# One ring of cells, held six tiles for U and seven for V instead of five and eight

## What is computed

```python
x = x + concat(RMSNorm(stick_breaking), RMSNorm(short_conv)) @ w_out
q1, q2 = split((RMSNorm(x) @ w_q) per head)            # 8 heads
s1, s2 = q1 @ sub_keys[0].T, q2 @ sub_keys[1].T        # 128 scores each
v1, i1 = top_k(s1, 16); v2, i2 = top_k(s2, 16)
top_s, pos = top_k(v1[:, None] + v2[None, :], 16)      # of 256 sums
idx = (i1 * 128 + i2)[pos]; gate = softmax(top_s)
act = gelu(sum_d expert_u[idx] * h)                    # one dot a pick
out = sum over picks of gate * act * expert_v[idx]
```

## Time and profile before

| what | us |
|---|---|
| median of the three runs | 2880.5 |
| the profiled execution, its own time | 2880.65 |
| its span (first to last instruction) | 2878.9 |
| POOL idle ahead of its DMAs, until a dot | 1372.7 |
| POOL idle ahead of its DMAs, until a mixed pair | 239.6 |
| PE, DVE, ACT, POOL busy | 2228.8, 1984.7, 1094.8, 1091.0 |

### The profile page before, as it was taken

How to read it: one execution, slowest core, us unless ns; L and a number is a source line. 1 busy time by engine, 2 the same in 40 slices (tenths; PEclk the granted TensorE clock), 3 DMA queues, 4 the chain that set the end, 5 groups by cost and what they waited for, 6 DMA issues and landing times. The chain is left out here.

```text
span 2878.9 us, 29484 instructions
## 1 busy us (share of the span) xinstructions
PE 2228.8 (77%) x9210; PEld 1015.9 (35%) x9210; DVE 1984.7 (69%) x4782; ACT 1094.8 (38%) x3164; POOL 1091.0 (38%) x1037
## 2 busy tenths in 40 slices
PE   9788989878987887778886888777898655555555
PEld 6535625433542343333442244333354111111111
DVE  3757766787666667787767666888676666666654
ACT  2323423562333336562333334666243332222232
POOL 0232423343333334443443333555333433333332
PEclk9999999889998998889998899999999787777786
DMA  9899999999999999999999999999999999999998
GB/s 389 331 418 404 402 420 418 417 412 410 394 421 421 419 419 399 421 421 419 409 422 421 420 411 418 404 414 418 418 412 421 417 422 421 420 420 417 419 416 353
DMA packets 178861, 1183.86 MB, mean 411 GB/s; under 512 B 19856, under 2 KB 21520, under 8 KB 47632
## 3 DMA queue, kind: packets, MB, share of 16 engines
q0 software_dynamic: 147456, 1073.81, 90.3%
q1 hardware_dynamic: 31248, 108.17, 9.5%
HBM read 1177.70 MB, written 4.19 MB: 411 GB/s over the span
## 5 line engine op out<-in xcount | busy, mean ns | idle before, releaser
L1470 DVE CUSTOM_DVE_ANT_0 ring<-ring,h2r 128x1024 f32<-128x1024 f32 x1024 | 1248.5, 1223 | 775.5 <-DMA ring<-table_uv,idx_t 768.3
L641 POOL DMA_INDIRECT ring<-table_uv,idx_t x1024 | 1089.1, 1064 | 1768.1 <-DVE dots L1470 1372.7
L909 PE MATMUL acc<-ring,wmask 128*64 128x512 f32 x4096 | 1202.2, 716 | 582.3 <-ACT wmask L1067 581.9
L909 PEld LDWEIGHTS acc<-ring,wmask 128*64 128x64 f32 x4096 | 283.2, 153 | 1293.3 <-ACT wmask L1067 856.5
L1062 ACT ACTIVATE dots<-dots 128x2 f32<-128x2 f32 x512 | 104.0, 203 | 1518.7 <-DVE dots L1470 1515.7
L1067 ACT ACTIVATE wmask<-gmask,dots 128x64 f32<-128x64 f32 x1024 | 300.4, 340 | 48.6 <-ACT dots L1062 1.5
L1055 ACT ACTIVATE gmask<-stack,gate_t 128x64 f32<-128x64 f32 x1024 | 293.1, 334 | 0.1
L664 PE MATMUL pt<-hT,w_held 128*128 128x256 f32 (+1 forms) x560 | 109.6, 345 | 0.0
L664 PEld LDWEIGHTS pt<-hT,w_held 128*128 128x128 f32 x560 | 88.4, 193 | 27.6 <-issue 20.2
L1062 ACT ACT_TABLE_LOAD x73 | 93.7, 1283 | 1.3
L655 PE MATMUL pz<-w_ring,hT 128*128 128x512 f32 x192 | 91.2, 618 | 0.0
(11 more groups left out here) (274 smaller groups left out, 2172.7 us busy)
## 6 DMA issues: line engine op xcount, KB each, us to landing
w_ring<-wstream SPq DMA_DIRECT2D x121, 512.0 KB
ring<-wstream SPq DMA_DIRECT2D x32, 512.0 KB, 11.5
ring<-table_uv,idx_t POOLq DMA_INDIRECT x1024
w_held<-wstream SPq DMA_DIRECT2D x11, 512.0 KB, 13.1
xs<-x_in_dram SPq DMA_DIRECT2D x8, 512.0 KB
h2r<-wstream SPq DMA_DIRECT2D x8, 512.0 KB, 14.4
scores<-wstream SPq DMA_DIRECT2D x8, 512.0 KB, 15.3
xs<-wstream SPq DMA_DIRECT2D x4, 512.0 KB, 11.6
```

The source lines that it names most:

```text
L641: nc.gpsimd.indirect_dma_start(out=ring[:, cell(t):cell(t) + 2, :].rearrange("p c d -> p (c d)"), out_offset=None, in_=table, in_offset=ba ...
L909: mm = nc.tensor.matmul(acc[HALF * i:HALF * i + HALF, half * 512:(half + 1) * 512], wmask[:, slot, :], ring[:, cell(2 * p + i) + 1, half * ...
L1470: V.tensor_tensor_reduce(u, u, h2r[:, b % H_SLOTS, i, :], 1.0, 0.0, ALU.mult, ALU.add, dots[:, t % SLOTS:t % SLOTS + 1]).then_inc(dots_don ...
```

## The change

```diff
-U_HOLD, V_HOLD = 5, SLOTS
+U_HOLD, V_HOLD = 6, 7
 TURN = U_HOLD + V_HOLD
 CELLS = TURN + 1
+RANK_BEGIN = 2
 def cell(t):
-    return U_HOLD * (t % TURN) % TURN
+    return -t * pow(U_HOLD, -1, TURN) % TURN
...
             start = QPICKS * r - RANK_LEAD
-            tick = start + k if start >= 0 else -1 + k * (QPICKS * r - 10) // RANK_TIME[-1]
+            tick = start + k if start >= 0 else RANK_BEGIN + k * (QPICKS * r - 10 - RANK_BEGIN) // RANK_TIME[-1]
...
-                if t % 2 == 0:
-                    wait(pool, pair_done, (t - V_HOLD) // 2 + 1)
-                wait(pool, dots_done, t - U_HOLD + 1)
+                wait(pool, pair_done, (t - V_HOLD) // 2 + 1)
+                if cell(t) + 2 < CELLS:
+                    wait(pool, dots_done, t - U_HOLD + 1)
```

## The result

The changed kernel took 2918.06 us (median of five runs, 2915.74 to 2932.85) against 2880.5 us beside it: ratio 1.0137, interval 1.012 to 1.0154. Forecast were 2890 us, in a range of 2877 to 2901. The sign was right; the loss is 37.6 us where 9.5 were forecast.

The account below looks back on a forecast made before the run. The prediction took the DMA engines to bound the kernel: bytes at 421 GB/s plus dry moments. Odd tiles' wait 9.0, even tiles 0, first fetches 0.5 and ranking 0 summed to 9.5 us of loss: 2890 us, range 2877 to 2901.

Parts of the forecast that it names:

- The bound: Whole kernel: time is the bytes at 421 GB/s plus dry moments of the DMA engines; POOL's waits cost nothing as such.
- The room: Ordinary stretches: an issue may be 4.77 us late at no cost, from 10.69 against 5.92 us issue to dot.
- The number of places: Late pairs where POOL idles over about 3.8 us: 9 places, at a mean of 1.0 us each.
- the dear rival: Where PE is behind for long, each odd tile runs dry anew: nine places at 2.49 us, 2903 us; chance 0.08.
- The term of 9.0 us: Odd tiles' new wait for a pair, the main term: loss of 9.0 us, bounds 0 and 22.4 us.
- The single place at 1098 us: Odd tile issued 7.55 us later behind a late pair; costs 1.7 us, any place at most 2.49 us.
- The even tiles' looser wait: Even tiles need the dot of t-6 in place of t-5; gains nothing, value 0.
- The first fetches: Start: seven tiles go in a row, the eighth waits for PE's first pair; loss 0.5 us, 0.7 as upper end.
- The ranking: Ranking moved by two ticks near the start: value 0; one step, 1.4 us, if DVE ended it late.
- Hidden after all: Engines don't all run dry at once, so only the three longest waits cost, 1 us each: 2883.5 us; chance 0.28.
- Faster: U half held for six tiles gives one more tile to ride out dry moments; 9.3 us gained, 2871; chance 0.12.
- The rule of the skill: A tile's fetch takes 4.4 us, giving 6.3 us of room and a sum of about 3 us; rejected for the row.

Follow-up runs that it names:

- e10: Kernel before, with odd tiles waiting for the pair of t-7 and t-6 only from tile 768 on; 2879.98 us, ratio 1.0.
- e9: Kernel before, with four chained small memsets on POOL between waits and issue from tile 7 on; 2891.24 us, ratio 1.0037.
- e3: Kernel before, with odd tiles also waiting for the pair of t-7 and t-6, on all tiles; 2910.26 us, ratio 1.01.
- e2: Changed kernel with the ranking put back to its old ticks; 2912.08 us, ratio 1.0112.
- e15: Kernel before, where a tile whose cells overwrite no U half (one in 13) waits for no dot; 2880.03 us, ratio 0.9996.
- e5: Changed kernel with even tiles waiting for the dot of t-5 again; 2915.11 us, ratio 1.0116.
- e14: Changed kernel with the ranking at its old ticks, run once more beside the changed kernel; 2915.16 us, ratio 1.0112.
- e1: Kernel before, with only the ranking moved (first part from tick -1 to tick 2); 2881.13 us, ratio 1.0005.
- e13: The changed kernel itself, measured and profiled once more; 2919.89 us, ratio 1.0132.
- e4: Kernel before, with every tile waiting for one dot more (t-4 in place of t-5); 2962.79 us, ratio 1.0284.

## Why the forecast was too low, step by step

**The bound: right.** The time is the DMA engines' in every kernel here, and POOL's waits as such cost nothing: 504.0 us for pairs in e10 are free.

**The room: the step that failed.** "The difference, 4.77 us, is what an issue may be late in an ordinary stretch at no cost." It compared a calm tile with one whose fetch found nothing ahead of it, and took all of the difference as free. Two things are wrong in it. It was read from issue to dot, while an engine runs dry as soon as first data is late. From issue to first data the two tiles have 5.49 and 1.67 us, a difference of 3.8; the other 0.95 lies behind the first data (5.20 and 4.25 us to the dot). And the packets show a price long before the queue is dry: they take longer once a tile is issued less than some 4.5 us ahead of its first data. With the usual lead of 5.54 us the room is about 1 us, an estimate from the lead table. e9, where the leads were 0.87 us shorter and 10 us were lost, bears it out, with POOL's slower pace as a part of unknown size.

**The number of places: wrong by the same step.** With 3.8 us of idle time as the threshold there were nine; with one microsecond of room nearly each late pair of the busy stretches would count, an inference that fits how the loss grows. The landings run behind before's by 4.7 us at tile 64, 13.8 at 256, 23.8 at 512, 33.6 at 736, and then stand still. It is in kind the dear rival ("each odd tile runs dry anew", 2903 us, a chance of 0.08), with slow packets on top. The term of 9.0 us measured 30.5 in e3. Its trace is 30.9 us longer than the one before; the accounts give 16.2 us of dry time, above the 9.0 and within the bound of 22.4, and 17.0 of slow packets, which the sum had at nothing.

**The single place at 1098 us: right in kind, low in size.** 2.7 us against 1.7, above the "at most 2.49". That bound was for one late tile, and the next odd tiles waited for PE there as well.

**The even tiles' looser wait: right.** e2 isn't faster than e3, e15 is level with before, and e5, with the stricter wait back, is level with the changed kernel.

**The first fetches: right in kind.** Eighth tile at 116.88 and released by PE. With the ranking back (e2, e14) tile 8 lands 0.7 and 0.9 us before its time in the kernel before; but e1 and e9, whose first fetches wait for what they waited for in that kernel, and e3, whose tile 7 already waits for the first pair, land it 1.3 to 1.9 before it. Against these the start costs some 0.8 us, where 0.5 was the value and 0.7 the upper end. That is no finer than the start itself: ACT's copy ahead of the first gelu stands at 108.33 in e9 and at 110.00 in e1.

**The ranking: 0 alone, open in the new order.** e1 bears the value out for the old waits. With the odd tile waiting for the pair, a dot that is late passes through the mask and PE to the next fetch, as tile 15 shows. "Value 0; if DVE had to end the ranking late, one step" looked at the end of the ranking, and this delay stands at its middle, in tick 9. By the medians the ranking costs some 5 us twice over (e2 against the changed kernel, e14 against e13), which the intervals don't settle, and in the traces of e13 and e14 the delay of 5.5 us at tile 32 is gone by tile 256.

**The rivals.** Hidden after all: no, the calm stretch alone is hidden (e10). Faster: no, as its rows said; the releaser at these places is PE.

**The rule of the skill.** The page of the Trainium skill that the prediction cites ("DMA: Bandwidth & Descriptors", section "Anatomy of one DMA") leads to 6.3 us of room, still further from the 1 us that the packets give. Both the row and the rule give the bare way of one fetch; neither says how early a fetch must be issued for its packets to run at full rate.

**What stays open.** Why packets take longer at a short lead: no run changed the making of descriptors or their layout, so no cause is claimed. The lead table tells what goes together over nine traces, not what causes what: a tile can be issued late because its forerunners landed late. Of the slower kernels only e9 made no wait stricter, and it changed POOL's pace too. The first and second executions of the changed kernel differ by 19 us, and why is not known. A larger delay by memsets wasn't tried, since POOL itself would have become the bound.

## What to carry to other kernels

Before a wait is moved to an earlier or stricter place on a queue that feeds a bandwidth-bound stream, take the lead of the present issues (start of issue to first data) from the trace, and look whether the rate falls where it is short, while the share still reads 1.00; only what lies above that lead is room. A wait for an engine that does other work, as PE here, passes that engine's delays on to the stream: 30.5 us in e3, and nothing where PE had little else to do (e10). Test the price of lateness by itself, with a small delay in the issuing queue, before a ring is split anew, and look that the delay leaves that queue able to catch up.

## What the runs showed of the hardware

- The DMA share near 1.00 does not tell the rate: 8 KB packets of the same fetch gave 422 GB/s and 332 GB/s at shares of 1.00 and 0.99 (windows of before at 1108 to 1112 us and of e4 at 1628 to 1632 us).
- The price of lateness is steep: e9 took the median from issue to first data down by 0.87 us and cost 10 us in all, e4 took it down by 1.42 us (5.54 to 4.12) and cost 83 us.
- Slow packets of a fetch stand mostly where one tile's packets end and the next one's begin: in e4 the first 16 and the last 32 of a tile's 128 packets have 64 of the 89 us.
- Issues 0.30 us apart, 558 of them, cost nothing that e5 could tell.
